# Joined attention: PE's linear scores and key turns ahead of the first turns, first linear chunk ahead of the next scores, first values ahead of the second turns

## The chip, the cores and the metric

The kernel runs on one core of a Trainium2 chip, as one launch. The metric is device time in microseconds (us), lower is better. The core's engines have their own queues, which run in order and meet at semaphores: PE (TensorE, matrix products and transposes), DVE (VectorE), ACT (ScalarE), POOL (GpSimd) and SP (SyncE, which issues most of the loads).

## The reference

The reference is two small transformer blocks over a sequence of 512 tokens of width 1024, in float32: first a gated-delta mixer with a gated feed-forward layer, then two layers with mixture-of-experts feed-forward. The change lies in the mixer of the first of these two layers (the "even" mixer). It computes two attentions side by side from the same projected input, with 8 heads of softmax attention in a sliding window, and 4 heads of gated linear attention:

```python
def _even_mixer(h, w_in, w_out, q_norm, k_norm, sinks, gate_up, gate_bias, out_norm, rel_bias):
    qa, ka, va, qb, kb, vb, rb, ab = jnp.split(h @ w_in, ...)
    oa = _swa_sink_attention(qa, ka, va, sinks, rel_bias)        # window, softmax with a sink
    log_a = jax.nn.log_sigmoid(ab @ gate_up + gate_bias) / B_GATE_TAU
    ob = _gla(qb, kb, vb, log_a)                                 # chunks of 64 tokens, carried state
    ob = _rms(ob, out_norm) * jax.nn.silu(rb)
    return jnp.concatenate([oa, ob], axis=-1) @ w_out
```

The window attention of a block of 128 queries looks at its own 128 keys and the 128 before. The linear attention carries a state per head from chunk to chunk: an output is the product of queries with the state so far, plus a masked product within the chunk.

## The kernel before, in words

The whole program keeps its data in one large on-chip tile, arena, and computes products into eight PSUM banks of 128 x 512. The program is a row of stages; each is a block with one hand-written sequence per engine. The order of the work on an engine is the order in which its sequence is written; the only links between engines are semaphores, waited for ahead of an instruction. The stage at issue is even_attention (L2101), called once by even_mixer. It lies between the projection of the even layer (project_all) and its output projection (project_out). There are no loads in it.

It joins the two attentions in a loop over four blocks n of 128 tokens. On PE a block has these steps:

- scores(n, pair) (products on L2135): window logits of four heads into banks 0 and 1; those of the next block, n + 1, are computed in block n. They wait until DVE has read the banks' former content.
- turn(n, q) (L2147), q = 0 to 3: transposes of two heads' shares, four of 128 x 128 (two in block 0), into bank 2 or 3. They wait for POOL's scaling of that half of the heads, and for the bank to be copied out.
- value(n, half) (L2159): products of values with turned shares into bank 4. They wait for the copies of the turned shares and for the output of the half before to be copied out.
- linear_scores(n) (L2170, and the key turns, L2176): products of keys and queries of the linear attention, and transposes of the decayed keys. They wait for the linear output of block n - 1 to be copied out (ACT, L2348) and for the last state update.
- linear_chunk(n, cc) (L2194, L2197, L2201), cc = 0, 1: output of a chunk of 64 tokens, and the state's increment into bank 7. The first waits for DVE's masked scores and key copy, each for the state of the chunk before.

DVE's sequence for block n is: shares (L2263, L2264, the reciprocal of the sums), logits(n + 1, 0) (L2246), copy of turn 0 (L2272), mask (L2279) and key copy (L2282), logits(n + 1, 1), state(n, 0) (L2294), copy of turn 2, peaks(n + 1) (L2254 to L2257, the row maxima of the next block), state(n, 1). ACT's is: copies of turns 1 and 3 (L2336), output of half 0 (L2342), powers(n + 1) (L2324, L2326, eight exponentials with their sums) or, in the last block, the silu of the gate (L2359), the linear output (L2348), output of half 1. POOL only scales the shares of block n by the reciprocal sums, in two halves (L2231), once DVE's shares(n) is through.

The fp32 products appear as two instructions each in the trace, the transposes as one.

Of the kernel before, what the change touches and what calls it, by code (L numbers as in the profile page):

```python
# [149 lines left out]
class Program:  # L150
# [1950 lines left out]
    def even_attention(self, qa, ka, va, band, vb, rb, o, free):  # L2101
# [23 lines left out]
        with nc.Block() as block:  # L2125
            @block.tensor
            def _(pe):
                def scores(n, pair):

                    lo = 0 if n else P  # L2130
                    if 2 * n + pair >= 1:
                        pe.wait_ge(s["lg"], 2 * n + pair)
                    for c in (2 * pair, 2 * pair + 1):
                        for half in range(2):
                            mm = pe.matmul(sc[half][:, c % 2, lo:], qa[rows[half], c, n * P:(n + 1) * P],  # L2135
                                           ka[rows[half], 0, (n - 1) * P + lo:(n + 1) * P], start=True, stop=True)
                    mm.then_inc(s["s"], 1)

                def turn(n, q):

                    pe.wait_ge(s["p"], 2 * n + q // 2 + 1)
                    if 2 * n + q // 2 >= 1:
                        pe.wait_ge(s["tk_odd"] if q % 2 else s["tk_even"], 2 * n + q // 2)
                    for i in range(4):
                        if i % 2 == 0 and n == 0:
                            continue
                        mm = pe.transpose(tb[q % 2][:, i, :], pbuf[n % 2][:, 2 * q + i // 2, (i % 2) * P:(i % 2 + 1) * P],  # L2147
                                          self.C("ident"))
                    mm.then_inc(s["t"], 1)

                def value(n, half):

                    pe.wait_ge(s["tk_even"], 2 * n + half + 1)
                    pe.wait_ge(s["tk_odd"], 2 * n + half + 1)
                    if 2 * n + half >= 1:
                        pe.wait_ge(s["ok"], 2 * n + half)
                    for hh in range(4 * half, 4 * half + 4):
                        for i in range(2) if n else [1]:
                            mm = pe.matmul(ob[:, hh % 4, :], va[:, n - 1 + i, :], pT[:, 2 * hh + i, :],  # L2159
                                           start=(i == (0 if n else 1)), stop=(i == 1))  # L2160
                    mm.then_inc(s["o"], 1)

                def linear_scores(b):

                    cols = slice(b * P, (b + 1) * P)
                    if b >= 1:
                        pe.wait_ge(g["ok"], b)
                    for c in range(2):
                        for half in range(2):
                            mm = pe.matmul(ab[half][:, c, :], kn[rows[half], c, cols], qd[rows[half], c, cols],  # L2170
                                           start=True, stop=True)
                    mm.then_inc(g["att"], 1)
                    if b >= 1:
                        pe.wait_ge(g["st"], 2 * b)
                    for c in range(2):
                        mm = pe.transpose(kb[:, c, :], kd[:, c, cols], self.C("ident"))  # L2176
                    mm.then_inc(g["kt"], 1)

                def linear_chunk(b, cc):

                    n = 2 * b + cc
                    if cc == 0:
                        pe.wait_ge(g["attk"], b + 1)
                        pe.wait_ge(g["kk"], b + 1)
                    if n >= 1:
                        pe.wait_ge(g["st"], n)
                    else:
                        pe.wait_ge(g["zero"], 1)
                    part = slice(64 * cc, 64 * cc + 64)
                    tok = slice(b * P + 64 * cc, b * P + 64 * cc + 64)  # L2190
                    for c in range(2):
                        for half in range(2):
                            hh = 2 * c + half
                            pe.matmul(lob[half][:, c, part], vb[:, b, hh * P:(hh + 1) * P],  # L2194
                                      att[b % 2][half][:, c, part], start=True, stop=False)
                        for half in range(2):
                            mm = pe.matmul(lob[half][:, c, part], St[rows[half], c, :], qd[rows[half], c, tok],  # L2197
                                           start=False, stop=True)
                    mm.then_inc(g["o"], 1)
                    for c in range(2):  # L2200
                        mm = pe.matmul(ub[:, c * 256:c * 256 + 256], kdn[b % 2][part, c, :],  # L2201
                                       vb[part, b, c * 256:c * 256 + 256], start=True, stop=True)
                    mm.then_inc(g["u"], 1)
# [3 lines left out]
                for n in range(4):  # L2207
                    if n + 1 < 4:
                        scores(n + 1, 0)
                    turn(n, 0)  # L2210
                    turn(n, 1)
                    linear_scores(n)
                    if n + 1 < 4:
                        scores(n + 1, 1)
                    linear_chunk(n, 0)
                    turn(n, 2)
                    turn(n, 3)
                    value(n, 0)
                    linear_chunk(n, 1)
                    value(n, 1)  # L2220

# [1207 lines left out]
```

## Time and profile before

| | |
|---|---|
| median of 3 runs | 3062.34 us (3058.05 to 3067.43) |
| the profiled execution's own time | 3065.07 us |
| its span in the trace | 3062.2 us |
| PE busy | 2802.9 us, 92% of the span |
| PE weight loads | 1806.0 us, 59% |
| DVE busy | 1486.6 us, 49% |
| ACT busy | 645.2 us, 21% |
| POOL busy | 157.8 us, 5% |
| mean granted clock | 0.955 |

The span is the time from the first to the last record of the core. Busy shares are those of the whole program; a stage can look quite different. The granted clock is TensorE's share of full speed: 1.00 is 2.4 GHz, 0.50 is 1.2 GHz. In a timeline a row is a run of like instructions with its start, its length, engine, line, operation, tiles and count, and in brackets the idle time of the engine before it with what ended it. An L-number is a line of the kernel.

### The profile page before, as it was taken

How to read it: one execution, taken by the hardware profiler on the slowest of the kernel's cores; microseconds unless marked ns; L12 is line 12 of the kernel's file. 1: busy time of each engine (PE TensorE's matmuls, PEld its weight loads, DVE VectorE, ACT ScalarE, POOL GpSimd, SP SyncE). 2: the span in 40 equal slices, each digit the busy share in tenths (PEclk: the TensorE clock that was granted, in tenths of full speed). 3: DMA queues.
4: the chain of work that ended last, by engine and by line, in shares of the span. 5: the costliest groups of instructions: out<-in, count | busy, mean ns of one | idle time of the engine just before them, and what ended most of it. 6: DMA issues, size and time to landing. Idle time of an engine off the chain costs nothing. (4 is left out here: it accounts for less than half of the span.)

```text
span 3062.2 us, 36633 instructions
## 1 busy us (share of the span) xinstructions
PE 2802.9 (92%) x14040; PEld 1806.0 (59%) x14040; DVE 1486.6 (49%) x2943; ACT 645.2 (21%) x1350; POOL 157.8 (5%) x169
## 2 busy tenths in 40 slices
PE   6989769999988999998979989999889898899998
PEld 4877657788946888886864533333278645333332
DVE  4567555566735667336542433333555634233334
ACT  3111454444531111001132200000102422000000
POOL 0000021222200000000010000000000000000000
PEclk8999989999998999999979899999999998999999
DMA  6111146664022232222202799999731035999998
GB/s 250 51 46 55 69 149 251 248 226 161 15 89 63 86 94 83 73 79 70 70 1 100 284 409 418 420 419 419 308 124 69 28 155 211 405 418 420 419 419 357
DMA packets 112918, 614.81 MB, mean 201 GB/s; under 512 B 12944, under 2 KB 13408, under 8 KB 62944
## 3 DMA queue, kind: packets, MB, share of 16 engines
q1 hardware_dynamic: 102464, 576.67, 48.6%
q0 software_dynamic: 9120, 31.49, 2.9%
q10 hardware_dynamic: 1152, 4.19, 0.3%
q8 instruction: 117, 1.92, 0.3%
q14 instruction: 65, 0.53, 0.1%
HBM read 603.79 MB, written 8.51 MB: 200 GB/s over the span
## 5 line engine op out<-in xcount | busy, mean ns | idle before, releaser
L2916 PE MATMUL bank<-arena 128*32 128x512 f32 (+2 forms) x2048 | 432.3, 604 | 14.2 <-DMA arena<-in_w 13.3
L440 PE MATMUL bank<-arena 128*128 128x256 f32 x1776 | 411.6, 386 | 33.6 <-DVE arena L493 10.8
L440 PEld LDWEIGHTS bank<-arena 128*128 128x128 f32 x1776 | 341.3, 193 | 100.3 <-issue 34.5
L2916 PEld LDWEIGHTS bank<-arena 128*32 128x32 f32 (+2 forms) x2048 | 148.9, 135 | 270.4 <-issue 269.4
L2940 PE MATMUL bank<-arena 128*32 128x512 f32 (+2 forms) x1024 | 226.0, 637 | 29.9 <-DMA arena<-in_w 28.2
L2954 PE MATMUL bank<-arena 128*128 128x512 f32 x480 | 235.2, 613 | 5.6 <-DVE arena L3070 1.8
L253 PE MATMUL bank<-arena 128*128 128x512 f32 (+1 forms) x608 | 217.2, 516 | 14.8 <-DVE arena L652 13.9
L3084 DVE SCALAR_TENSOR_TENSOR arena<-bank,arena 128x512 f32<-128x512 f32 x240 | 180.3, 751 | 77.0 <-PE bank L2954 64.2
L253 PEld LDWEIGHTS bank<-arena 128*128 128x128 f32 x608 | 119.1, 197 | 110.1 <-issue 101.5
L2940 PEld LDWEIGHTS bank<-arena 128*32 128x32 f32 (+2 forms) x1024 | 78.0, 140 | 174.2 <-issue 171.8
L2954 PEld LDWEIGHTS bank<-arena 128*128 128x128 f32 x480 | 76.5, 188 | 161.8 <-DVE arena L3084 96.5
L3002 ACT ACTIVATE arena<-bank 128x512 f32<-128x512 f32 x30 | 17.9, 598 | 511.6 <-PE bank L2899 487.3
L3091 DVE TENSOR_TENSOR arena<-arena,bank 128x512 f32<-128x512 f32 x30 | 20.6, 688 | 204.8 <-ACT arena L3026 204.8
L3070 DVE COPY arena<-bank 128x512 f32<-128x512 f32 x30 | 20.7, 692 | 201.8 <-PE bank L2940 201.8
L1475 PE MATMUL bank<-arena 128*128 128x256 f32 x528 | 118.3, 379 | 0.0
L1111 ACT ACTIVATE arena<-bank 128x256 f32<-128x256 f32 x288 | 93.6, 383 | 87.7 <-PE bank L1031 65.2
L1475 PEld LDWEIGHTS bank<-arena 128*128 128x128 f32 x528 | 100.2, 190 | 14.8
L1031 PE MATMUL bank<-arena 128*128 128x128 f32 x576 | 99.0, 295 | 1.5 <-DVE arena L1226 0.8
L1031 PEld LDWEIGHTS bank<-arena 128*128 128x128 f32 x576 | 76.1, 192 | 39.7 <-issue 31.2
L1223 DVE TENSOR_TENSOR arena<-bank,arena 128x256 f32<-128x256 f32 x144 | 60.9, 423 | 76.5 <-PE bank L1016 76.3
L1016 PE MATMUL bank<-arena 128*128 128x128 f32 x576 | 94.6, 287 | 0.6
L3059 DVE COPY arena<-bank 128x512 f32<-128x512 f32 x26 | 18.0, 692 | 145.0 <-PE bank L2899 145.0
(455 smaller groups left out, 4135.5 us busy)
## 6 DMA issues: line engine op xcount, KB each, us to landing
arena<-in_w SPq DMA_DIRECT2D x384, 1024.0 KB, 19.5
arena<-in_dense SPq DMA_DIRECT2D x308, 512.0 KB, 4.5
arena<-core_rows POOLq DMA_DIRECT2D x48, 256.0 KB, 6.5
arena<-in_xT SPq DMA_DIRECT2D x2, 2048.0 KB, 12.6
token_rows<-arena ACTq DMA_DIRECT2D x8, 512.0 KB, 3.9
gdn_gate<-arena POOLq DMA_DIRECT2D x8, 256.0 KB, 2.6
arena<-gdn_gate SPq DMA_DIRECT2D x1, 2048.0 KB, 8.3
arena<-band_bias POOLq DMA_DIRECT2D x2, 1024.0 KB, 6.1
```

The lines of the kernel that those rows point to most:

```text
L253: mm = eng.matmul(dst, w[:, k, :], src[:, k, :], start=(k == 0), stop=(k == KD - 1))
L440: mm = pe.matmul(out, w[:, k, :], x[:, k, :], start=(k == 0), stop=(k == K1 - 1))
L1016: mm = pe.matmul(Y[u][:, q, :], buf[u]["bl"][:, q, :], buf[u]["xl"][:, u, q, :], start=True, stop=True)
L1031: mm = pe.matmul(touched(X[u][:, 2 * q:2 * q + 2, :], l, u), buf[u]["zs"][:, q, :], buf[u]["yn"][:, q, :], start=False, stop=(l == 6), ski ...
L1111: act.activation(gathered(buf[u]["xl"][:, side, :, :], l + 1), touched(X[u], l + 1, side), ACT.Copy).then_inc(kept, 1)
L1223: dve.tensor_tensor(buf[u]["yn"], Y[u][:, 0:2, :], levels[:, l - 1, :, :].to_broadcast([P, 2, P]), ALU.mult).then_inc(s["yn"], 1)
L1475: mm = pe.matmul(product(m, p), s4[:, t, k, :], ht[:, t, k, :], start=(k == 0), stop=(k == K1 - 1))
L2916: mm = pe.matmul(self.bank[2 + t][part, :], xT[i % 2][:, 2 * q + k, part], w[j][:, k, t, :], start=(q == 0 and k == 0), stop=(q == 3 and k ...
L2940: mm = pe.matmul(self.bank[7 - t][part, :], aT[:, k, part], w[j][:, k, :], start=(k == 0), stop=(k == 3))
L2954: pe.matmul(self.bank[4 + k % 2][:, :], y[i % 2][:, k * P:(k + 1) * P], scatter[i % 2], start=True, stop=True).then_inc(s["summed"], 1)
L3070: dve.tensor_copy(y[i % 2][:, 512:1024], self.bank[6][:, :]).then_inc(s["yk0"], 1)
L3084: dve.scalar_tensor_tensor(self.x[:, k, :], self.bank[4 + k % 2][:, :], gate[:, k:k + 1], self.x[:, k, :], ALU.mult, ALU.add).then_inc(s[" ...
```

## The change

Within each of the four blocks PE's steps are written in another order. In block n, the linear scores with their key turns come before the first two turns (they came after them); the first linear chunk comes before the next block's second scores (it came after them); the first values come before the third and fourth turns (they came after them). The steps themselves, their waits, and the sequences of DVE, ACT and POOL are as they were.

```diff
                 for n in range(4):
                     if n + 1 < 4:
                         scores(n + 1, 0)
+                    linear_scores(n)
                     turn(n, 0)
                     turn(n, 1)
-                    linear_scores(n)
+                    linear_chunk(n, 0)
                     if n + 1 < 4:
                         scores(n + 1, 1)
-                    linear_chunk(n, 0)
+                    value(n, 0)
                     turn(n, 2)
                     turn(n, 3)
-                    value(n, 0)
                     linear_chunk(n, 1)
                     value(n, 1)
```

## Rows read from the trace of the kernel before

**Rows 1.** Windows: stage, us, busy (count) of PE, PEld, DVE, ACT, POOL; PEclk, DMA share, GB/s.
```profile
1526.60:1617.50 90.90, 72.39 (x432) 57.70 (x432) 41.09 (x93) 30.14 (x94) 13.28 (x8) 0.74 0.00 1
```
**Rows 2.** Waits in that stage: who waited for whom, us in total, times, longest.
```profile
PE bank L2147 <- POOL arena L2231: 15.4, 4, 4.5
```
**Rows 3.** Timeline of block n = 1, PE's products.
```profile
1553.17 1.14 PE L2135 MATMUL bank<-arena 64*128 64x256 f32 x8
...
1557.86 1.97 PE L2147 MATMUL bank<-arena 128*128 128x128 f32 x8 [3.56 <-POOL arena L2231]
1559.76 1.23 PE L2170 MATMUL bank<-arena 64*128 64x128 f32 x8
...
1561.54 1.99 PE L2135 MATMUL bank<-arena 64*128 64x256 f32 x8
1563.46 0.66 PE L2194 MATMUL bank<-arena 128*128 128x64 f32 x4
...
1566.29 1.10 PE L2147 MATMUL bank<-arena 128*128 128x128 f32 x8
1567.23 1.95 PE L2159 MATMUL bank<-arena 128*128 128x128 f32 x16
1569.01 0.56 PE L2194 MATMUL bank<-arena 128*128 128x64 f32 x4
```
**Rows 4.** Timeline of the same block, DVE.
```profile
1559.02 0.69 DVE L2272 COPY arena<-bank 128x512 f32<-128x512 f32 x1 [1.86 <-PE bank L2147]
...
1563.58 1.29 DVE L2246 SCALAR_TENSOR_TENSOR arena<-bank,arena 128x512 f32<-128x512 f32 x2 [1.46 <-PE bank L2135]
1566.40 1.44 DVE L2294 SCALAR_TENSOR_TENSOR arena<-arena,bank 64x128 f32<-64x128 f32 x4 [1.53 <-PE bank L2201]
```
**Rows 5.** Timeline of the same block, ACT and POOL, to POOL's next start.
```profile
1555.31 0.63 ACT L2348 ACTIVATE arena<-bank 128x256 f32<-128x256 f32 x2
1555.91 3.75 POOL L2231 TENSOR_TENSOR arena<-arena 128x1024 f32<-128x1024 f32 x2 [18.52 <-DVE arena L2264]
...
1576.05 3.75 POOL L2231 TENSOR_TENSOR arena<-arena 128x1024 f32<-128x1024 f32 x2 [16.39 <-DVE arena L2264]
```
**Rows 6.** Timeline of block 0 (five rows) and of the last block, n = 3.
```profile
1536.45 1.12 PE L2147 MATMUL bank<-arena 128*128 128x128 f32 x4 [4.54 <-POOL arena L2231]
1537.18 0.42 DVE L2272 COPY arena<-bank 128x256 f32<-128x256 f32 x1 [0.75 <-PE bank L2147]
1537.50 1.23 PE L2170 MATMUL bank<-arena 64*128 64x128 f32 x8
...
1541.28 1.12 PE L2194 MATMUL bank<-arena 128*128 128x64 f32 x4
...
1546.43 1.12 PE L2147 MATMUL bank<-arena 128*128 128x128 f32 x4
...
1598.26 1.97 PE L2147 MATMUL bank<-arena 128*128 128x128 f32 x8 [4.20 <-POOL arena L2231]
1599.41 0.69 DVE L2272 COPY arena<-bank 128x512 f32<-128x512 f32 x1 [3.18 <-PE bank L2147]
1601.44 0.76 DVE L2279 TENSOR_TENSOR arena<-bank,arena 128x256 f32<-128x256 f32 x2 [1.33 <-PE bank L2170]
1602.11 0.41 DVE L2282 COPY arena<-bank 128x256 f32<-128x256 f32 x1
1602.62 1.09 PE L2194 MATMUL bank<-arena 128*128 128x64 f32 x4 [0.61 <-DVE arena L2279]
```
**Rows 7.** Windows within the stage: columns as in rows 1; PEclk is the third from the end.
```profile
1536.40:1549.30 12.90, 12.85 (x56) 9.95 (x57) 5.49 (x13) 0.78 (x3) 0.99 (x1) 0.50 0.00 0
1557.80:1563.00 5.20, 5.14 (x26) 3.97 (x26) 1.78 (x4) 0.60 (x1) 1.86 (x2) 0.50 0.02 3
1563.50:1574.80 11.30, 11.30 (x90) 9.60 (x88) 7.47 (x15) 4.60 (x16) 0.00 (x0) 1.00 0.00 0
1604.20:1610.90 6.70, 6.70 (x29) 5.68 (x28) 2.09 (x5) 0.60 (x1) 0.00 (x0) 0.50 0.01 2
```

## The prediction

> **What bounds the kernel now.** The page's head says that PE is busy for most of the span, so PE's queue is the usual bound. But an average over stages says little here, because the change touches one stage only, the joined attention of the even layer. The windows view puts that stage at 90.90 us, 3.0% of the span of 3062.2, with PE busy 72.39 us (80%), DVE 41.09, ACT 30.14, POOL 13.28, no DMA to speak of and a mean granted clock of 0.74 [rows 1]. So no engine is full: it is a chain from engine to engine. The waits view then shows what PE's idle time is: the first turns (L2147) wait for POOL's scaling (L2231), 15.4 us in four pieces [rows 2].
>
> The timeline of the block n = 1 gives the chain. POOL starts its two products at 1555.91; the first turns start on PE at 1557.86, when the first product is in; then PE runs without a gap: turns to 1559.76, the linear scores with the key turns to 1561.54, the next block's second scores to 1563.46, the first linear chunk to 1566.29 [rows 3, 5]. 0.11 us later DVE runs the state update (L2294, to 1567.84) [rows 4], then its copy of turn 2 and the peaks of the next block; then ACT has the powers, DVE the shares, and POOL starts the next block at 1576.05 [rows 5]. That is a cycle of 20.14 us. All that PE does between the release of the first turns and the end of the first linear chunk is on it; the second turns, the values and the second chunk are not, since PE is through with them and idle again before the next release. In the last block there is no next block, and PE's own queue carries the end: turns from 1598.26, linear scores, a wait of 0.61 for the mask, then chunks and values [rows 6].
>
> **The change, part by part.** Nothing is added or removed: no instruction, no DMA, no wait. Only PE's order within a block changes; the orders of DVE, ACT and POOL stay. That is what decides here.
>
> (a) The linear scores and key turns go ahead of the first turns. They wait for ACT's copy of the linear output (L2348) of the block before, which ends at 1555.31 + 0.63 = 1555.94 [rows 5], and for the state, done by then. So they can run from about 1556.05, and take 1.78 us at the low clock (1559.76 to 1561.54): to 1557.83, before the release at 1557.86 [rows 3]. They are hidden, with next to no margin. I cost them at nothing; the upper bound is their whole 1.78 us if the release is lost on them. In block 0 PE idles 4.54 us and they wait for nothing, so there the cover is ample [rows 6]. Gain: 1.78 us in each block.
>
> (b) The first linear chunk now follows the first turns directly. It needs the masked scores (L2279) and keys (L2282) from DVE, and on DVE these are queued behind the copy of turn 0 (L2272), which needs the first turn. So having the linear scores early gives DVE nothing to do before that copy's end. In block 1: copy 1559.02 + 0.69 = 1559.71 [rows 4]; then 0.03 of hand-over, mask and key copy, which take 1.08 together (1601.44 to 1602.11 + 0.41 = 1602.52), and 0.10 from DVE to PE (1602.52 to 1602.62), 1.21 in all [rows 6]. The chunk starts at 1560.92, against the turns' end at 1559.76: a new PE wait of 1.16. Before, the next block's scores covered it. Block 2 repeats block 1. In block 0 turns and copy are half as many: 1537.18 + 0.42 + 1.21 = 1538.81, less 1537.50, is 1.31 [rows 6].
>
> (c) The next block's second scores now follow the chunk. On DVE their logits (L2246) stand ahead of the state update. Before, these logits ran under the chunk, free. Now the state update has to wait for scores and logits: from the scores' end 0.12 + 1.29 + 0.03 = 1.44 us pass until it can start, where it had been 0.11 behind the chunk [rows 3, 4]. Cost: 1.33 us on the cycle in each of blocks 0, 1 and 2. Chunk and scores have merely changed places on PE, so their own durations cancel.
>
> (d) The first values go ahead of turns 2 and 3. Off the cycle: after the scores' end the values take 1.78 (1567.23 to 1569.01) and turn 2 half of 0.94, together 2.25, while DVE is busy for 2.88 with logits and state before it wants turn 2 [rows 3, 4]. Cost and gain nothing while the clock is high. ACT's order (turns 1 and 3, output, powers) isn't hurt either: what it needs is in before the peaks end. The second chunk may wait some tenths for the state; its cover is the idle time at the block's end, 3.56 us and the like [rows 3].
>
> Sum on the cycle: block 0: 1.31 + 1.33 - 1.78 = +0.86; blocks 1 and 2: 1.16 + 1.33 - 1.78 = +0.71 each. In the last block (c) doesn't exist: the chunk starts at 1599.41 + 0.69 + 1.21 = 1601.31 where it had started at 1602.62, so -1.31, and PE's queue carries that to the end [rows 6]. Together 0.86 + 0.71 + 0.71 - 1.31 = +0.97 us. Everything after the stage (output projection, router, the expert loads issued behind it) starts with it and moves by the same amount.
>
> The sum is made on a profiled span of 3062.2 us, whose own time was 3065.07; the median of three runs is 3062.34. I add it to the median: 3063.3.
>
> **The clock, the unknown in it.** The granted clock is 0.50 (1.2 GHz) from 1536.4 to 1549.3, 0.50 again in 1557.8 to 1563.0, 1.00 (2.4 GHz) from 1563.5 to 1574.8, and 0.50 in 1604.2 to 1610.9 [rows 7]. Between the blocks it fell while PE stood idle for POOL. The first chunk takes 2.83 us at the high level and 5.15 at the low (1541.28 to 1546.43) [rows 3, 6]. My sum lets every piece keep the level that it had. If the clock rises at the same instant as before, the chunk, now earlier, does 2.4 us of work at the low level and the scores run at the high: +0.2 in blocks 1 and 2, and some +0.6 in the last. So the forecast case spans 3062.5 to 3065.
>
> **Rivals.**
>
> *The clock stays low (slower).* In block 1 it rose behind turns, linear scores and wide scores without a gap; in the last block, where PE went from turns and linear scores into a wait of 0.61 and the narrow chunk, it was still low 12.6 us after the turns began [rows 3, 6, 7]. The new order makes blocks 1 and 2 look like the last: turns, a wait of 1.2, the chunk. Price for each: the chunk, 5.15 less 2.83 = +2.32; and now (d) bites: values at the low level take twice 1.78 = 3.56 and turn 2 half of 1.90, 0.95, with 0.11 to DVE 4.62, against DVE's 2.91: +1.71. With the +0.71, +4.7 for a block. One block: some 3067. Both, with the tail as before: 0.86 + 9.5 - 1.31 = +9.0, 3071.4. With the last block low to its end, where second chunk and values would lose about what the first ones do (2.3 + 1.8): +13, 3075.5. It decides from the point at which the clock doesn't come back under the first chunk. Against it: the linear scores now fill part of the idle time, and turns follow them without a gap.
> The Trainium skill, "TensorE: Matmul & The Clock Gate", Part 4, says that transposes don't count as PE activity for the clock; by that the turns do nothing to bring it back, and the result is this rival. No row here separates turns from the products around them.
>
> *The clock is kept through the wait (faster).* The linear scores cut the idle piece in two, 1.7 us and next to none. Then in blocks 1 and 2 the turns take 0.94 instead of 1.90; the chunk starts 2.57 after the release (first turn 0.47, some 0.2 to DVE, copy 0.69, 1.21), and the state update at 2.57 + 2.83 + 1.14 + 1.44 = 7.98, where it was at 1566.40 - 1557.86 = 8.54: -0.56 each [rows 3, 4]. Block 0 would give 2.1 + 2.83 + 1.14 + 1.44 = 7.5 against 1546.54 - 1536.45 = 10.1, -2.6. The last block has 12.6 us at the low level, 2.3 of them linear scores and wait; the other 10.3 halve, and a wait of 1.6 comes: 6.8 against 12.6, -5.8 [rows 6, 7]. All four: -9.5, 3052.8; one or two of them, the likelier: 3056 to 3061. Against it: PE is idle from 1554.31, and by 1557.8 the clock had dropped; the linear scores can't start before 1556.05 [rows 3, 5, 7].
> The Trainium skill, same page, section "Why this matters for your kernels", advises to keep idle gaps between bursts short, or the clock falls back. By that rule this rival holds and the change is a gain of the size just worked out.
>
> *The change hides nothing:* the linear scores still come too late and delay the turns. That would add up to 1.78 in blocks 1 and 2: 3066.8. The copy's end at 1555.94 speaks against more than 0.1 [rows 5].
>
> **Chances.** Forecast case 0.60 (3062.5 to 3065); low clock 0.22, of it 0.06 beyond +9.2; kept clock 0.13, of it 0.02 beyond -9.2; hiding fails 0.05. The three runs before lie between 3058.05 and 3067.43, so a median can be off by 2 or 3 us, and a measurement can tell about 0.3%, 9.2 us. The range goes from two kept blocks, less some of that spread, to nearly the two low blocks: 3057 to 3070. With the spread: faster by over 0.3% 0.03, within 0.90, slower 0.07.
>
> **What would show it.** Linear scores (L2170) start some 0.1 after L2348 ends and end before L2147 starts; PE has a new wait of about 1.2 for DVE's L2282 ahead of L2194 in every block; L2294 follows L2246 without a gap; POOL's starts lie some 20.9 apart instead of 20.14; the stage takes 91 to 93 us, its mean clock still near 0.74. I am wrong if POOL's starts come closer together, if the clock reads 0.50 for most of blocks 1 and 2 (starts near 25 apart), or if the stage keeps its length and the total moves.

## The result, and the profile after

The changed kernel takes 3070.73 us in the median of 22 runs (3064.22 to 3078.79), the kernel before in the same comparison 3062.88 (3058.05 to 3071.72). The ratio is 1.0021, 95% interval 1.0014 to 1.0027: slower, by 0.21%, some 6.4 us by the ratio and 7.9 by the medians. Ratios are over the undisturbed executions: one of the twelve of a later run, the wide scores computed twice, took 7419.45 us and is not in them. The profiled execution took 3074.40 us, its span is 3071.8.

The windows of the changed kernel, split at the stage's last product: in and behind the stage. Columns as in rows 1.

```profile
1527.50:1625.90 98.40, 77.08 (x432) 63.82 (x432) 40.13 (x93) 29.68 (x94) 13.29 (x8) 0.71 0.00 1
1625.90:3071.80 1445.90, 1335.40 (x5602) 621.59 (x5602) 560.84 (x1043) 189.67 (x352) 32.02 (x32) 0.97 0.76 307
```

The stage takes 98.40 us where it had 90.90 [rows 1], with a mean granted clock of 0.71 instead of 0.74; ahead of it the program takes 1527.50 instead of 1526.60, behind it 1445.90 instead of 1444.70. So 7.5 of the 9.6 us between the two profiled spans are in the stage.

Its waits show where, in the columns of rows 2:

```profile
DVE arena L2246 <- PE bank L2135: 22.3, 5, 7.0
PE bank L2170 <- ACT arena L2348: 8.3, 3, 3.2
PE bank L2147 <- POOL arena L2231: 5.9, 4, 3.5
PE bank L2194 <- DVE arena L2279: 4.0, 4, 1.1
```

In the kernel before, DVE's wait for the second scores was small:

```profile
DVE arena L2246 <- PE bank L2135: 5.8, 5, 1.5
```

The turns' wait for POOL fell from 15.4 us [rows 2] to 5.9; 8.3 of it now stand ahead of the linear scores. Two waits have grown: PE's for DVE's mask, once 0.61 before [rows 6] and now four times about 1; and DVE's for the second scores, from at most 1.5 to up to 7.0 us, with the state update queued behind it.

POOL's starts, block 1 to the last, are the clearest measure of the cycle:

```profile
1557.08 3.75 POOL L2231 TENSOR_TENSOR arena<-arena 128x1024 f32<-128x1024 f32 x2 [18.82 <-DVE arena L2264]
1581.08 3.75 POOL L2231 TENSOR_TENSOR arena<-arena 128x1024 f32<-128x1024 f32 x2 [20.24 <-DVE arena L2264]
1605.02 3.75 POOL L2231 TENSOR_TENSOR arena<-arena 128x1024 f32<-128x1024 f32 x2 [20.19 <-DVE arena L2264]
```

They lie 24.00 and 23.94 us apart, and the first of them 20.86 behind block 0's. In the kernel before the three distances are 20.56, 20.14 [rows 5] and 20.26. So block 0 is 0.3 us longer, and blocks 1 and 2 are longer by 3.9 and 3.7, where 0.71 was forecast. PE's timeline of block n = 1, which answers to rows 3:

```profile
1557.15 0.71 PE L2170 MATMUL bank<-arena 64*128 64x128 f32 x8 [2.91 <-ACT arena L2348]
...
1559.03 1.97 PE L2147 MATMUL bank<-arena 128*128 128x128 f32 x8 [0.79 <-POOL arena L2231]
1561.97 1.08 PE L2194 MATMUL bank<-arena 128*128 128x64 f32 x4 [0.97 <-DVE arena L2279]
...
1566.69 2.17 PE L2135 MATMUL bank<-arena 64*128 64x256 f32 x7
1568.79 3.63 PE L2159 MATMUL bank<-arena 128*128 128x128 f32 x16
```

The linear scores start at 1557.15, are short (the clock is still high), and are over before the turns' release at 1559.03. Then the turns, a wait of 0.97, and the first chunk, from 1561.97 to some 1567, all of it at the low clock: about 5 us where it had taken 2.83 [rows 3]. The wide scores (2.17 for seven) and the values (3.63 for sixteen, against 1.95) are at the low clock too. DVE's side, which answers to rows 4:

```profile
1561.45 0.41 DVE L2282 COPY arena<-bank 128x256 f32<-128x256 f32 x1
1568.91 1.29 DVE L2246 SCALAR_TENSOR_TENSOR arena<-bank,arena 128x512 f32<-128x512 f32 x2 [7.04 <-PE bank L2135]
1570.12 1.43 DVE L2294 SCALAR_TENSOR_TENSOR arena<-arena,bank 64x128 f32<-64x128 f32 x4
1572.89 0.69 DVE L2272 COPY arena<-bank 128x512 f32<-128x512 f32 x1 [1.34 <-PE bank L2147]
```

The logits wait 7.04 us for PE, the state update follows them at once, and the copy of turn 2 waits another 1.34, because values and turn 2 are slow. The windows of the granted clock, columns as in rows 1, PEclk third from the end:

```profile
1559.00:1572.00 13.00, 12.00 (x51) 10.25 (x52) 4.27 (x10) 0.60 (x1) 1.83 (x1) 0.50 0.01 1
1573.00:1581.00 8.00, 5.97 (x47) 4.81 (x45) 4.95 (x11) 5.66 (x21) 0.00 (x0) 1.00 0.00 0
```

In block 1 the clock is at 0.50 from the turns to nearly the end of the values, 13 us, and in block 2 the same (1583 to 1596); in the kernel before it was back at 1.00 when the chunk began [rows 7].

### The profile page after: what moved, and what is told of

It reads as the page before. It is cut to its first block and busy times, and to the rows that moved or that the text cites. A ratio compares the mean times of both kernels' runs of the same rounds, so it can differ in the third digit from the quotient of the medians.

```text
span 3071.8 us, 36633 instructions
## 1 busy us (share of the span) xinstructions
PE 2811.8 (92%) x14040; PEld 1812.7 (59%) x14040; DVE 1485.6 (48%) x2943; ACT 645.2 (21%) x1350; POOL 158.0 (5%) x169
```

## The experiments

Theory A: the cost of the order itself is what the prediction summed, about 1 us, and the rest is the low clock, which stays because after the turns PE now meets a wait and the first chunk, whose products are called narrow below (128x64 in the rows), instead of the second scores, called wide (64x256). Theory B: hiding the linear scores is itself what loses the clock, or the order costs 4 us a block at any clock.

Stage length below means from the stage's first product to the first one of the output projection: 91.09 us in the kernel before, 98.51 in the changed one. Ratios are against the kernel before on the same chip. One profiled execution stands for each kernel where no second is named. The diffs leave out the conditions around the next block's steps, and `...` marks what is left out between two pieces.

**Linear scores moved alone**

```diff
                     scores(n + 1, 0)
+                linear_scores(n)
                 turn(n, 0)
                 turn(n, 1)
-                linear_scores(n)
```

> Only the linear scores and key turns go ahead of the first turns; the first chunk stays behind the next block's wide scores, the values behind turns 2 and 3. Theory A (the clock stays low because the narrow first chunk, with a DVE wait ahead of it, follows the turns): here turns and wide scores still follow each other without a gap, so the clock comes back as in the kernel before; 1.78 us leave the cycle in blocks 0 to 2 and some 1.3 in the last: POOL's starts 18.4 apart instead of 20.14, stage 84 to 85 us instead of 90.9, total some 6.5 us under the kernel before (3056). Theory B (hiding the linear scores is itself what keeps the clock low): turns, scores, chunk and values low, POOL's starts 23 or more apart, total over 3066.

Ratio 0.9971 (0.9960 to 0.9982), 8.9 us less by the ratio; stage 86.85 us; POOL's starts 18.97, 17.81 and 21.01 apart. PE in block 1:

```profile
1554.42 0.81 PE L2170 MATMUL bank<-arena 64*128 64x128 f32 x8
...
1555.44 1.04 PE L2147 MATMUL bank<-arena 128*128 128x128 f32 x8
1556.41 1.14 PE L2135 MATMUL bank<-arena 64*128 64x256 f32 x8
1557.87 0.63 PE L2194 MATMUL bank<-arena 128*128 128x64 f32 x4 [0.32 <-issue]
```

Linear scores, turns, wide scores and chunk follow each other with one pause of 0.32, all at the high clock, so this block is shorter than the forecast 18.4, although the linear scores are not hidden in it: PE was late, and the turns start 0.9 us behind POOL's release. In block 2 the clock stayed low into the values, and it is longer. Block 2's window:

```profile
1572.00:1585.50 13.50, 13.12 (x55) 10.78 (x56) 6.84 (x12) 1.19 (x2) 2.18 (x2) 0.50 0.01 1
```

Theory B falls in its first form as an account of the total: hiding the linear scores is a gain, and the order in which they are hidden without the other moves is the best of the three. But in block 2 what it foresaw is there: turns, wide scores straight behind them, chunk and most of the values all ran at 0.50, without a wait in between. So wide scores behind the turns do not bring the clock back every time. The total fell by twice what the stage did in this profile (4.2 us); the profiled execution was the slowest of the seven, and where the rest came from is not shown.

**First chunk moved alone**

```diff
                 turn(n, 1)
                 linear_scores(n)
+                linear_chunk(n, 0)
                 scores(n + 1, 1)
-                linear_chunk(n, 0)
```

> The linear scores stay behind the first turns; the first chunk goes ahead of the next block's second scores; values stay behind turns 2 and 3. Theory A: a wait of 0.6 to 1.0 for DVE's mask ahead of the chunk, scores and logits on the cycle (+1.33), and the chunk at the low clock (+2.32) in blocks 1 and 2: POOL's starts 24 to 25 apart, stage near 101 us, total some 10 us over the kernel before (3073). Theory B (the clock is lost through the hidden linear scores): only +2.0 a block, starts 22.2 apart, total +6 (3069).

PE in block 1, and POOL's starts of blocks 1 and 2:

```profile
1562.56 0.69 PE L2176 MATMUL bank<-arena 128*128 128x128 f32 x2
1563.87 1.09 PE L2194 MATMUL bank<-arena 128*128 128x64 f32 x4 [0.61 <-DVE arena L2279]
```

```profile
1557.56 3.75 POOL L2231 TENSOR_TENSOR arena<-arena 128x1024 f32<-128x1024 f32 x2 [20.09 <-DVE arena L2264]
1581.67 3.75 POOL L2231 TENSOR_TENSOR arena<-arena 128x1024 f32<-128x1024 f32 x2 [20.36 <-DVE arena L2264]
```

The wait of 0.61 for the mask and a low chunk are there (1.09 for its first four instructions, 0.66 in rows 3), and the starts lie 22.13, 24.11 and 24.11 apart, as theory A has it; stage 99.29 us. But the total did not follow: ratio 1.0005 (0.9987 to 1.0022). So it ran again:

> The kernel with only the first chunk moved ahead of the next scores, again: its stage was 99.3 us, 8 longer than before, yet its total equal. If the total follows the stage on average: +5 us or more over the kernel before this time, and a rest of the program near 1444 as in the others. If something behind the stage gives it back every time: total +0 again and a rest near 1437.

Ratio 1.0008 (0.9997 to 1.0019); stage 94.89, starts 22.14, 20.94 and 22.04 apart. Two things are mixed here: the stage's length depends on how the clock falls in an execution, and the rest of the program was shorter both times, 1437.1 and 1440.3 us against 1444.4 in the kernel before. A part of that has a place. The windows of 14 us that begin 80 us behind the stage's end (the router): the kernel before

```profile
1697.78:1711.78 14.00, 12.38 (x83) 12.14 (x82) 10.16 (x20) 1.51 (x4) 0.00 (x0) 0.76 0.50 184
```

and, of the kernel with the first chunk moved alone, its first execution

```profile
1706.06:1720.06 14.00, 11.84 (x95) 10.86 (x94) 11.36 (x27) 2.60 (x6) 0.62 (x1) 1.00 0.50 185
```

and its second:

```profile
1698.41:1712.41 14.00, 11.84 (x95) 10.84 (x94) 11.36 (x27) 2.60 (x6) 0.64 (x1) 1.00 0.50 186
```

The router runs at 0.76 in the kernel before and at 1.00 in both executions of this one, and the experts' first products then start 3.0 us earlier, 92.8 us behind the stage's end instead of 95.8. The changed kernel's router runs at 0.76. So neither expectation fits: the rest is not near 1444, and the return is not complete. Some 3 us come back in the router; what else differs lies in later stages and wasn't followed up. In the second execution the first chunk of blocks 1 and 2 ran at the high clock (0.63 for its first four instructions), with a wait of 0.61 and 0.71 right ahead of it: so wait and narrow chunk don't keep the clock low every time either.

**First values moved alone**

```diff
                 linear_chunk(n, 0)
+                value(n, 0)
                 turn(n, 2)
                 turn(n, 3)
-                value(n, 0)
```

> Only the first values go ahead of turns 2 and 3. Both theories: the clock is as before. DVE's copy of turn 2 follows chunk, values and turn 2 (1.78 + 0.47 + 0.1 = 2.35 us after the chunk) where it followed the state update (1.58): +0.8 on the cycle of blocks 1 and 2, some +0.5 in block 0: POOL's starts 20.9 apart, total +2 us (3065). If values are off the cycle altogether: starts 20.14 apart, total +0.

Ratio 1.0008 (0.9999 to 1.0017). Starts 17.89, 21.21 and 20.89 apart; stage 91.37. Blocks 1 and 2 are 1.1 and 0.6 us longer than before, around the forecast 0.8: without the logits on the cycle, the values ahead of turn 2 do delay DVE's copy. Block 0 was short, since in that execution the clock came back early. The total doesn't exclude zero.

**DVE's order fitted to PE's** (against the changed kernel)

```diff
                 shares(n)
                 logits(n + 1, 0)
-                turned(n, 0)
                 masked(n)
+                turned(n, 0)
+                state(n, 0)
                 logits(n + 1, 1)
-                state(n, 0)
```

> The changed kernel's PE order, with DVE's order fitted to it: mask and key copy ahead of the copy of turn 0, state update ahead of the next logits. No arithmetic is changed. The wait ahead of the chunk goes and the state update runs under the scores. If it was the wait of 1 us that kept the clock low: the clock is back under the chunk, the cycle is 1.0 shorter than before, starts 19.1 apart, total -5 us (3058). If it is the narrow chunk itself that doesn't bring the clock back: chunk, scores, values and turn 2 low, starts near 23.7 apart, total +3.5 us (3066.5).

PE in block 1, and the window with its granted clock:

```profile
1558.41 1.91 PE L2147 MATMUL bank<-arena 128*128 128x128 f32 x8 [0.80 <-POOL arena L2231]
1560.11 0.96 PE L2194 MATMUL bank<-arena 128*128 128x64 f32 x4
```

```profile
1558.60:1568.70 10.10, 10.10 (x45) 8.72 (x45) 3.46 (x8) 0.60 (x1) 1.61 (x1) 0.50 0.01 2
```

The chunk starts right behind the turns, without any wait; and turns, chunk and scores are still at 0.50, 10 us long. Ratio 0.9983 (0.9971 to 0.9995), stage 91.46, starts 19.12, 21.85 and 22.85 apart. So in this execution the clock stayed low without the wait. The loss in blocks 1 and 2 (1.7 and 2.6 us against before) is of the kind forecast for "the narrow chunk itself", though smaller. The total, -5 us by the ratio, is better than the stage, whose length is that of before; here too the router ran at 1.00 (rest of the program 1437.7).

**Wide scores computed twice** (against the changed kernel; `False` leaves out the signal)

```diff
                 turn(n, 1)
+                scores(n + 1, 1, False)
                 linear_chunk(n, 0)
                 scores(n + 1, 1)
```

> The changed kernel with the next block's second wide scores computed twice: once more, without their signal, ahead of the first chunk, where DVE's mask is waited for. If it is the missing wide products behind the turns that leave the clock low: the clock comes back under the chunk as in the kernel before, starts 20.8 apart, total +0 to +2 over the kernel before although PE does more. If the clock stays low in any case: chunk low and 0.8 us more work, starts near 25, total over +10.

PE in block 1 (lines past L2137 are one or two higher here), and POOL's starts of blocks 1 and 2:

```profile
1560.34 2.08 PE L2135 MATMUL bank<-arena 64*128 64x256 f32 x8
1562.35 0.84 PE L2195 MATMUL bank<-arena 128*128 128x64 f32 x4
1563.12 0.44 PE L2198 MATMUL bank<-arena 64*128 64x64 f32 x4
1563.49 0.66 PE L2195 MATMUL bank<-arena 128*128 128x64 f32 x4
```

```profile
1556.49 3.75 POOL L2234 TENSOR_TENSOR arena<-arena 128x1024 f32<-128x1024 f32 x2 [19.66 <-DVE arena L2267]
1577.19 3.75 POOL L2234 TENSOR_TENSOR arena<-arena 128x1024 f32<-128x1024 f32 x2 [16.96 <-DVE arena L2267]
```

More work for PE, and a shorter cycle: the starts lie 20.70 and 20.29 apart (21.70 in block 0) where the changed kernel had 24.00 and 23.94. The chunk starts low (0.84) and is back at the high clock from its second products on (0.44, 0.66). Ratio 0.9993 (0.9977 to 1.0009), which doesn't overlap the changed kernel's 1.0014 to 1.0027; stage 91.52. With the extra wide products between turns and chunk, which also fill the wait, the clock comes back in both blocks. It is one profile, though, and its router ran at 1.00 (rest of the program 1440.6), so a part of the gain over the changed kernel lies behind the stage in this profile.

What the clock did can be counted over the blocks 1 and 2 of the eleven profiles of kernels without filler (the repeats below with them), where it was low as the turns ran. Back within 6 us of the first turn's start: 6 of 6 blocks with both steps at their old places, 2 of 4 with only the first chunk moved, 2 of 3 with the linear scores early and wide scores still behind the turns (this run and the linear scores alone), 1 of 6 with the linear scores early and the chunk right behind the turns. The order bears on the clock, but it doesn't fix it, and these counts don't tell which of the two moves weighs more. When the clock fell is a third thing that differed: 1.0 to 1.4 us ahead of the turns in the kernel before, 0.6 to 0.7 in the first profile of the changed one, 1.6 and 2.1 in the second. No run held it fixed.

**Filler in the idle time, under both orders**

```diff
+                def warm(n, count):
+                    if n >= 1:
+                        pe.wait_ge(s["tk_even"], 2 * n)
+                    for i in range(count):
+                        pe.matmul(self.bank[2][:, :], self.C("ident"), self.x[:, i, :], start=True, stop=True)
...
                     scores(n + 1, 0)
+                warm(n, 3 if n else 2)
                 turn(n, 0)
```

> The kernel before with filler in PE's idle time ahead of the first turns: three wide products (two in block 0) of the identity with the residual tile into bank 2, whose content is then overwritten by the first turns; the result is unchanged. Theory A (the low clock after the idle time costs turns, linear scores and wide scores half their speed): the clock stays high in blocks 1 and 2 and those 5.6 us shrink to about 3.2, POOL's starts 17.7 apart instead of 20.14, total -6 us or more. If the filler doesn't hold the clock: starts 20 to 21 apart, total +0 to +2.

PE ahead of block 2's turns (L2210 is the filler):

```profile
1570.59 2.85 PE L2210 MATMUL bank<-arena 128*128 128x512 f32 x6
1573.81 1.10 PE L2147 MATMUL bank<-arena 128*128 128x128 f32 x8 [0.37 <-POOL arena L2239]
```

Ratio 0.9935 (0.9921 to 0.9949), stage 79.74 us, starts 19.62, 17.65 and 17.64 apart, the last two as worked out. The clock, from block 1 to the stage's end:

```profile
1547.20:1605.60 58.40, 53.45 (x374) 40.56 (x372) 31.08 (x69) 26.09 (x75) 11.24 (x6) 1.00 0.00 1
```

Filler in the idle time took 11.35 us off the 91.09. The low clock of block 0 is not in this: there it stayed at 0.50 for 13.6 us in two pieces. The total fell by some 20 us by the ratio, far more than the stage; the profiled execution was the slowest of the six, its rest of the program no shorter than before (1447.2), and where the other 9 us came from is not shown.

In the changed kernel two filler products stand ahead of the linear scores in every block:

```diff
                     scores(n + 1, 0)
+                warm(n, 2)
                 linear_scores(n)
```

> The changed kernel with the same filler, two wide products ahead of the linear scores in every block. It shows the new order with the clock taken out. Theory A (order alone costs little, most of the loss is the low clock under the first chunk): POOL's starts 19.5 apart instead of 24.0, that is some 1.8 us a block more than w_before (new wait 1.55 + logits 1.33 - linear scores 1.1), total 2 to 4 us over w_before and 5 to 7 under the changed kernel. Theory B (the order itself costs 4 us a block, whatever the clock): starts 23 to 24 apart.

PE's chunk in block 1, and the windows around the clock's fall:

```profile
1560.35 0.63 PE L2194 MATMUL bank<-arena 128*128 128x64 f32 x4 [1.39 <-DVE arena L2287]
...
1562.14 1.21 PE L2201 MATMUL bank<-arena 64*128 64x256 f32 x3
```

```profile
1556.00:1562.40 6.40, 4.22 (x35) 3.44 (x36) 2.84 (x6) 1.16 (x2) 3.67 (x2) 1.00 0.01 3
1562.60:1569.30 6.70, 6.70 (x29) 5.77 (x29) 2.59 (x6) 0.00 (x0) 0.00 (x0) 0.50 0.00 0
```

Ratio 0.9990 (0.9978 to 1.0003), stage 89.34, starts 19.01, 22.10 and 21.99. The expectation of 19.5 with the clock out of the way was wrong, since it wasn't out of the way: turns and the chunk's first half ran high, and then, behind the wait of 1.39 and the narrow products, the clock fell to 0.50 at 1562.5, with no idle time longer than 1.4 us in the 9 us before. In block 0 the fall came near the chunk's end, at 1542.0, and 19.01 is the cycle there. So with the clock high at the turns, this order with two filler products still lost it. That it is the order which loses it is not shown: two filler products didn't hold the clock in the last run below either, which keeps the wide scores behind the turns, and three were not tried here.

**Both kernels again**

The changed kernel, with POOL's starts from block 1 on:

> The changed kernel again, for a second profile of it and for its total on one chip beside the next kernel. If the low clock under the first chunk belongs to the order: low through chunk and scores again, POOL's starts 23.5 to 24 apart, stage 97 to 99 us, total +6 us. If it was an accident of one profiled execution: starts 20.9 apart, stage 92.

```profile
1554.13 3.75 POOL L2231 TENSOR_TENSOR arena<-arena 128x1024 f32<-128x1024 f32 x2 [18.83 <-DVE arena L2264]
1575.02 3.75 POOL L2231 TENSOR_TENSOR arena<-arena 128x1024 f32<-128x1024 f32 x2 [17.15 <-DVE arena L2264]
1598.30 3.75 POOL L2231 TENSOR_TENSOR arena<-arena 128x1024 f32<-128x1024 f32 x2 [19.53 <-DVE arena L2264]
```

Ratio 1.0023 (1.0012 to 1.0033), the result repeated. But the profile differs: starts 20.88, 20.89 and 23.28 apart, stage 94.41. In block 1 the chunk ran at the high clock, behind its wait:

```profile
1559.02 0.63 PE L2194 MATMUL bank<-arena 128*128 128x64 f32 x4 [1.00 <-DVE arena L2279]
```

That is the block of my sum, and it has its length. So the low chunk is not in every block of every execution, and theory B falls in its second form too: the order alone does not cost 4 us a block.

The kernel before, in the same way:

> The kernel before, unchanged, for a second profile of its stage. If the clock comes back under turns, linear scores and wide scores as a rule: stage 89 to 92 us, POOL's starts about 20.1 to 20.3 apart, first chunk of blocks 1 and 2 at the high clock. If the first profile was a lucky one: chunk low in a block, starts near 22.5 there, stage 93 or more. Total ratio 1.000 within 0.1%.

```profile
1551.63 3.75 POOL L2231 TENSOR_TENSOR arena<-arena 128x1024 f32<-128x1024 f32 x2 [18.51 <-DVE arena L2264]
1571.80 3.75 POOL L2231 TENSOR_TENSOR arena<-arena 128x1024 f32<-128x1024 f32 x2 [16.42 <-DVE arena L2264]
1592.08 3.75 POOL L2231 TENSOR_TENSOR arena<-arena 128x1024 f32<-128x1024 f32 x2 [16.53 <-DVE arena L2264]
```

20.56, 20.17 and 20.28 apart, stage 91.14: the same as the first profile within 0.05 us. In both the clock fell 2.5 us behind the stage's start and again at 29.8 to 29.9. In the changed kernel's two profiles that first fall lies at 3.6 us (stage 98.5) and 2.5 us (stage 94.4), in those of the chunk moved alone at 3.5 (99.3) and 2.5 (94.9). So at the same fall as in the kernel before, the changed one is 3.3 us longer; at the other, 7.4. How long the kernel before takes at the other fall, no profile here shows. Ratio of the kernel to itself 0.9990 (0.9980 to 1.0001): that is how exact these totals are, and differences of 0.1% between kernels are not told apart here.

**Two versions that beat both kernels**

The first is meant to take the chunk and the state update off the cycle. Against the kernel before, PE's and DVE's orders:

```diff
                     scores(n + 1, 0)
+                linear_scores(n)
                 turn(n, 0)
                 turn(n, 1)
-                linear_scores(n)
                     scores(n + 1, 1)
-                linear_chunk(n, 0)
                 turn(n, 2)
                 turn(n, 3)
                 value(n, 0)
+                linear_chunk(n, 0)
                 linear_chunk(n, 1)
...
                     logits(n + 1, 1)
-                state(n, 0)
                 turned(n, 2)
                     peaks(n + 1)
+                state(n, 0)
                 state(n, 1)
```

> Linear scores ahead of the turns, wide scores straight behind them, turns 2 and 3 and first values ahead of the first chunk; on DVE the copy of turn 2 and the next peaks ahead of the first state update. The chunk and the state update leave the cycle: by the rows of before (POOL 1.95, turns 1.90, scores 1.92, logits 1.41, copy 0.72, peaks 2.8, powers 4.2, shares 0.5) the cycle is 15.4, and PE's own work sets it at 17 to 18. POOL's starts 17 to 18 apart, total -8 to -11 us (3053). If the state update is late for the second chunk by more than the gain: starts 19 or more, total -3 or less.

Ratio 0.9967 (0.9952 to 0.9982); stage 84.35, starts 16.42, 18.60 and 20.32 apart. The gain is as forecast, the regularity isn't: the second chunk of blocks 1 and 2 now waits 1.5 us for the state, and the clock falls there.

The second combines filler (two products) with the linear scores moved alone:

```diff
                     scores(n + 1, 0)
+                warm(n, 2)
+                linear_scores(n)
                 turn(n, 0)
                 turn(n, 1)
-                linear_scores(n)
```

> Filler of two wide products in PE's idle time, the linear scores ahead of the first turns, and the next block's wide scores kept between turns and first chunk. With the clock high the cycle is that of w_before (17.65) less the linear scores at the high clock (1.0): POOL's starts 16.6 apart, stage some 76 us, total 3 us under w_before (3045). If two products don't hold the clock: starts 18.5, stage 82 to 86, total 3052.

Ratio 0.9944 (0.9923 to 0.9964), stage 78.17, starts 15.39, 16.99 and 18.20 apart. Two products don't hold the clock throughout (it fell at 1555.5 and at 1589.6). Its total can't be told from that of the kernel before with three filler products, 0.9935; its stage is 1.6 us shorter.

## Why the prediction was right or wrong

The direction is right, and the range, 3057 to 3070, just holds the move by the ratio (3062.34 times 1.0021 is 3068.8); the median itself lies 0.7 above it. That the move stays within 0.3% is right too. The forecast +1 us is too small: measured are 6 to 8. That the range holds is in part luck: the result lies outside the forecast case (3062.5 to 3065), and the range reached so far only because it was stretched towards a rival held for less likely. Point by point:

- (a) held. The linear scores start within 0.1 us of ACT's copy, take 1.1 us at the high clock, not 1.78, and end 0.8 us ahead of the release. In block 1 of the second profile they took 1.7 at the low clock and still ended 0.2 ahead.
- (b) held: a wait of 0.97 in three blocks and 1.13 in block 0, forecast 1.16 and 1.31. Of the 0.2 too much, 0.11 is DVE's hand-over: mask and state update start 0.08 before the instruction ahead ends, where I had put 0.03 after it.
- (c) held: the state update follows the logits without a gap. It starts 1.33 us behind the scores' end (1568.79 to 1570.12), forecast 1.44.
- (d) held where most of the values ran at the high clock (block 1 of the second profile: no wait), and its reversal at the low one too: DVE's copy waited 1.34 and 1.30 us for turn 2, forecast 1.71.
- The sum of the cycle in block 1, 20.14 + 0.71 = 20.85, is what the repeated profile shows, 20.89. Block 0 grew by 0.3 only (20.56 to 20.86 and 20.88), forecast 0.86; of that, some 0.3 is that the chunk's last products and the first scores overlap on PE, 6.82 us for both at the low clock (1539.56 to 1546.38) where they had taken 7.1 one after the other.
- The failed step is "my sum lets every piece keep the level that it had". I had the low-clock rival with its mechanism, pieces and price (+4.7 a block; 3.9, 3.7 and 3.0 measured) and with the row that pointed to it, the last block of the kernel before, where a wait and the chunk follow turns and linear scores. I gave it 0.22. It came in three of the four blocks 1 and 2 that the two profiles of the changed kernel show. In block 0 it costs nothing, because there the chunk was low before as well.
- The last block: -1.31 forecast, -0.41 and -0.77 measured (21.47 from POOL's last start to the stage's end, then 21.06 and 20.70). The chunk started 1.4 us earlier against the release (forecast 1.31), but the clock stayed low as long behind it, to 12 to 13 us after the turns began, so that more of the work behind the chunk fell under it.
- The rival of a kept clock did not come. Its rule, from the Trainium skill ("TensorE: Matmul & The Clock Gate", section "Why this matters for your kernels": keep idle gaps between bursts short), is not enough by the runs here: with gaps of at most 1.4 us, the filled version of the changed order lost the clock in the middle of the chunk. What the Trainium skill says of transposes (the same title, Part 4) was not separated by any run.

What is shown is that the low clock under chunk, scores and values makes the difference: the same order had a block of 20.89 us with the chunk at the high clock and blocks of 23.3 to 24.0 with it low. What stays open is why the clock stays low: whether the narrow products, the wait ahead of them, the early linear scores or the moment at which the clock falls weighs most. Without the wait the clock stayed low too, and with wide products in it, it came back; a run with a wait and wide products wasn't made, and neither were repeats of these two.

## What to carry to other kernels

Before moving a small step into an idle gap, look at what then stands first behind the gap. Here PE met a wait and the narrow chunk there instead of the wide scores, the clock that the gap had cost stayed away longer in most blocks, and they grew by 3.0 to 3.9 us where a step of 1.78 was to be hidden. Move a step together with the steps on the other engines that are queued for it: here PE had its linear scores early, while DVE, its order unchanged, made the mask at the same place in its queue as ever. And undo or redo each of several moves alone: of the three, one alone is worth -9 us, the other two alone move the total by less than these runs can tell, and all three together cost 6 to 8.

## What the runs showed of the hardware

- With filler products in PE's idle time the clock stayed at 1.00 from block 1 to the stage's end, and the stage took 79.74 us instead of 91.09, although PE did more.
- A busy PE can stand at the low clock for long. In the changed kernel PE is busy 12.00 of the 13.00 us between 1559 and 1572, with only the linear scores moved 13.12 of the 13.50 between 1572 and 1585.5, and the clock is at 0.50 all the while.
- Where the clock's first fall lies against the stage's start takes few values (2.5 or 3.6 us in all eleven profiles of kernels without filler), and the two kernels profiled at both differ with it: 98.5 and 94.4 us for the changed one, 99.3 and 94.9 with the first chunk moved alone.
- 80 us behind the stage's end the router ran at 0.76 in some kernels and at 1.00 in others, 3 us apart, in the same way in both profiles of each of the three kernels that have two. That the stage's end passes this on is likely, but no run shows it. The whole rest of the program behind the stage, the same in every kernel, took from 1437.2 to 1449.4 us in the fourteen profiles. So a stage's change and the total's can differ by several microseconds, though nothing else was edited.
